# A hybrid decoder trunk: the sliding-window group's norm applied behind the output projection, its tiles placed between the last stick-breaking heads, and a new order at the MLP's opening and end

## The chip, the cores and the metric

The kernel runs on one core of one Trainium2 chip. The metric is the device time of one execution in microseconds (us): the median of three plain runs. Beside them stands one execution taken by the hardware profiler, whose trace is read below. The engines are TensorE (PE; PEld is its weight load), VectorE (DVE), ScalarE (ACT), GpSimd (POOL) and SyncE (SP), which issues nearly all DMAs.

## The reference

Two layers over 512 positions of width 1024, all in float32. In each:

```python
h = rmsnorm(x, attn_norm[l])
proj = h @ w_in[l]                      # sb_q, sb_k, sb_v (8 heads), sw_q (8 heads), sw_k, sw_v (2 heads), 64 wide
sb_o = stick_breaking_attention(...)    # z = q k / 8; a = exp(log_sigmoid(z) + suffix sums of -softplus(z)); a @ v
sw_o = sliding_window_sink_attention(...)   # rotary, window 128, softmax with sinks
mix = concatenate([rmsnorm(sb_o, sb_norm[l]), rmsnorm(sw_o, swa_norm[l])])
x = x + mix @ w_out[l]
h = rmsnorm(x, mlp_norm[l])
x = x + square(relu(h @ w_up[l])) @ w_down[l]
```

and a last rmsnorm. An rmsnorm divides every position (a column, below) by the root of its mean square and multiplies every channel by a gain.

## The kernel before

x lies in SBUF transposed, as 8 chunks of 128 channels by 512 positions. Every product is made of three float32r matmuls on a split of both operands into a high and a low part: high x high, high x low, low x high. A weight tile is loaded by DMA ("raw"), its high part is written by ScalarE, its low part by GpSimd. An operand's high part is written by ScalarE, its low part by VectorE. A dense tile is one PSUM bank of 128 x 512; the output projection's tiles take 12 matmuls each (4 chunks x 3).

The norms of the attention input, of the stick-breaking group and of the MLP are applied behind their products: only the gain goes into the operand, and the result is multiplied by 1/rms of its position, a [128, 512] tile made by a matmul with minus_one over summed squares, Ln and Exp on ScalarE and a refinement on VectorE. The sliding-window (SWA) group alone is normed ahead of its product: MN multiplies its four chunks osw by rms_w.

Each layer's attention part is a hand-written order of steps (ORDER_0, ORDER_1). Each engine walks the whole list and carries out its own steps, in the list's order, so the list is at once the queue of every engine; semaphores tie the queues together. The steps that matter, with a number for the tile, head half or chunk:

- T, U (TensorE): the first and second half of an input tile. TE, TH, TL (VectorE, ScalarE, VectorE): scale it, its high part, its low part. VT, VH, VL: the same for a transposed V tile. In layer 1 tile 17 is the query of heads 6 and 7; in layer 0 it is their V.
- BS, BX, BA (TensorE, L802 to L832): scores, suffix sums and output of the stick-breaking heads. Head h has the halves 2h (768 columns) and 2h+1 (512 columns) for BS and BX, and one BA. Between BS and BX lie BE (ScalarE, Abs, Exp, Ln), BP (VectorE), BH (ScalarE) and BL (VectorE); between BX and BA lie XE, XH (ScalarE) and XL (GpSimd). BO (ScalarE) and BD (VectorE) join the output; GH and GL (L1152, L1578) split it into mix_sb.
- SQ, SA: squares of the SWA group and their sum. NW0, NWE0, NWD0, NWF0: its norm's matmul, Ln and Exp, mean, refinement into rms_w. NS0 and so on: the same for the stick-breaking group, into rms_a.
- MN (VectorE, L1616): osw times rms_w. MH (ScalarE, L1182) and ML (VectorE, L1619): high and low part of chunk n of the SWA group, times its gain. The low part lies in the place of osw.
- OS (TensorE, L836 to L847): one of the 8 output tiles of the SWA group. OE (VectorE, L1625): its add into x.
- CH, CL: the high and low parts of weight pack n; at CL, SyncE also issues the load of pack n+2.

Head 7's scores take the banks of DW (z_last), so BS14 waits until the norm sum NW0 has been read, and BS15 for one of the dense banks. After the list come the 8 output tiles of the stick-breaking group, from mix_sb (on VectorE a multiply by rms_a in PSUM, L1630, a drain, and the add, L1632).

The MLP's order is written likewise (MLP_OPEN, MLP_PAIR, MLP_ON). PL: the 8 plain up tiles; PR, PQ, UH, UL: their relu, square and split. NM, NE, ND: the MLP's norm. MC, MH, ML: sums of activations for a fast scheme that the other up tiles use, and their split. KQ, KP and the other K steps: weight splits on ScalarE and GpSimd; LQ, LU, LD: their loads on SyncE. DF and DE or DX: a down tile and its add into x; DF3 takes the bank that DE0 frees. XC: the next layer's operand and the squares of a chunk. In layer 0's end KN0 to KN2 split the next layer's first weights.

## Time and profile before

| | us |
|---|---|
| median of three plain runs | 1172.91 (1172.42 to 1173.19) |
| profiled execution, own time | 1174.64 |
| its span, first to last instruction | 1172.9 |
| TensorE matmuls busy | 1139.7 |
| TensorE weight loads busy | 995.1 |
| VectorE busy | 829.1 |
| GpSimd busy | 714.2 |
| ScalarE busy | 659.6 |
| granted TensorE clock, mean | 0.994 of 2.4 GHz |

A busy time is the sum of an engine's instructions; matmuls overlap, so a matmul row of 0.39 us can be followed by the next after 0.23. A row of a timeline gives start, duration (of all it merges), engine, line and operands, and in brackets the idle time of the engine before it with what ended that. A name with "q" is the engine's sequencer. Layer 0's attention part ends at about 244 us, its MLP at 588; layer 1's attention part ends at about 818.

### The profile page before, as it was taken

To read this page: it belongs to the slowest core of one execution; us is meant where nothing else is said; L and a number is where in the kernel's file an instruction comes from. 1 tells how busy PE (TensorE), PEld (TensorE's weight loads), DVE (VectorE), ACT (ScalarE), POOL (GpSimd) and SP (SyncE) were. 2 spreads that over 40 slices of the span, in tenths; PEclk is the share of its full clock that TensorE was granted. 3 is DMA by queue.
4 is the path that set the end of the run, shared out by engine and by line. 5 is a ranking of instruction groups with operands and counts; after the bars stand their busy time and mean duration, and the time that the engine had idled before them with its cause. 6 is when DMAs were issued, how large, how long until landed. Compare 5 with 4: busy or idle time off the path is not lost.

```text
span 1172.9 us, 17809 instructions
## 1 busy us (share of the span) xinstructions
PE 1139.7 (97%) x6410; PEld 995.1 (85%) x6410; DVE 829.1 (71%) x1119; ACT 659.6 (56%) x1134; POOL 714.2 (61%) x430
## 2 busy tenths in 40 slices
PE   7999998999999999999999999899999999999996
PEld 5789887877899999989788889788878999999986
DVE  6766677687767778675755766767777877777755
ACT  6789898464344444443546888875643444444333
POOL 3454753674777768774754555556656877767733
PEclk9999998999999999999999999999999999999999
DMA  5220310422242322322222111114323232332222
GB/s 190 73 70 21 91 37 19 144 90 90 90 127 85 109 96 91 126 78 86 67 75 74 54 55 55 37 36 127 108 74 125 90 127 76 104 109 91 86 59 72
DMA packets 30055, 100.01 MB, mean 85 GB/s; under 512 B 3600, under 2 KB 5648, under 8 KB 29968
## 3 DMA queue, kind: packets, MB, share of 16 engines
q1 hardware_dynamic: 28992, 97.80, 26.4%
q8 instruction: 51, 0.84, 0.3%
q10 hardware_dynamic: 976, 1.08, 0.3%
q14 instruction: 36, 0.29, 0.1%
HBM read 96.77 MB, written 2.10 MB: 84 GB/s over the span
## 4 chain that ended last, share of the span: by engine, by line
PE 78%; ACT 8%; DVE 6%; issue 2%; ACTq 1%; DVEq 1%; POOL 1%; DMA 1%; POOLq 0%; SPq 0%
PE DW L672 27%; PE Z L649 5%; PE Z L648 5%; PE Z L647 5%; PE DW L639 5%; PE DW L641 5%; PE DW L640 5%; PE Z L639 3%; PE Z L641 3%; PE Z L640 3%; PE Z L819 2%; PE DW L753 2%; PE DW L649 1%; PE DW L648 1%; PE DW L647 1%
## 5 line engine op out<-in xcount | busy, mean ns | idle before, releaser
L672 PE MATMUL DW<-stage,wx 128*128 128x512 f32 (+1 forms) x816 | 193.3, 388 | 1.6 <-POOL wx L1283 1.6
L672 PEld LDWEIGHTS DW<-stage,wx 128*128 128x128 f32 x816 | 148.6, 188 | 30.2 <-POOL wx L1283 2.0
L672 PE MATMUL DW<-stage,w 128*128 128x512 f32 (+1 forms) x720 | 171.2, 387 | 2.0 <-DVE x L1694 2.0
L672 PEld LDWEIGHTS DW<-stage,w 128*128 128x128 f32 x720 | 130.8, 188 | 27.6 <-DVE x L1694 2.9
L1271 POOL TENSOR_TENSOR w<-raw,w 128x1024 fp32r<-128x1024 f32 x49 | 120.2, 2461 | 53.5 <-ACT w L957 49.7
L1692 DVE TENSOR_TENSOR DW<-DW,probs 128x512 f32<-128x512 f32 x122 | 85.1, 697 | 77.8 <-PE DW L672 74.1
L1289 POOL TENSOR_TENSOR w<-wsum,w 128x512 fp32r<-128x512 f32 x72 | 104.2, 1448 | 42.5 <-ACT w L995 42.5
L639 PE MATMUL DW<-xa,w 128*128 128x512 f32 x296 | 119.3, 403 | 9.4 <-DVE xa L1406 7.2
L1283 POOL TENSOR_TENSOR w<-raw_more,w 128x1024 fp32r<-128x1024 f32 x30 | 73.2, 2441 | 76.8 <-ACT w L977 76.6
L1283 POOL TENSOR_TENSOR wx<-raw_more,wx 128x1024 fp32r<-128x1024 f32 x34 | 82.6, 2433 | 59.1 <-ACT wx L977 58.9
L641 PE MATMUL DW<-xa,w 128*128 128x512 f32 x296 | 116.2, 393 | 0.0
L640 PE MATMUL DW<-xa,w 128*128 128x512 f32 x296 | 116.1, 392 | 0.0
L1289 POOL TENSOR_TENSOR w<-raw,w 128x512 fp32r<-128x512 f32 x60 | 91.4, 1538 | 0.7 <-ACT w L995 0.7
L1694 DVE TENSOR_TENSOR x<-DW,x 128x512 f32<-128x512 f32 x122 | 84.4, 692 | 9.4 <-issue 0.4
L649 PE MATMUL Z<-xm,w 128*128 128x256 f32 x288 | 81.5, 283 | 0.0
L648 PE MATMUL Z<-xm,w 128*128 128x256 f32 x288 | 81.5, 283 | 0.0
L647 PE MATMUL Z<-xm,w 128*128 128x256 f32 x288 | 81.2, 282 | 0.0
L1336 POOL TENSOR_TENSOR stage<-work,stage 128x768 fp32r<-128x768 f32 (+1 forms) x32 | 50.9, 1595 | 44.5 <-ACT stage L1138 43.8
L1429 DVE TENSOR_TENSOR wsum<-raw 128x512 f32<-128x512 f32 x48 | 71.8, 1496 | 7.1 <-issue 4.9
L639 PEld LDWEIGHTS DW<-xa,w 128*128 128x128 f32 x296 | 56.0, 189 | 22.5 <-issue 10.5
L1345 POOL TENSOR_TENSOR probs<-probs,small 128x1024 f32<-128x1024 f32 (+1 forms) x16 | 27.3, 1705 | 74.9 <-DVE small L1597 74.9
L1220 ACT ACTIVATE stage<-kf 128x512 fp32r<-128x512 f32 x64 | 40.6, 634 | 51.6 <-DVE kf L1677 25.6
(327 smaller groups left out, 3104.0 us busy)
## 6 DMA issues: line engine op xcount, KB each, us to landing
raw<-in_weights SPq DMA_DIRECT2D x115, 512.0 KB, 3.7
raw_more<-in_weights SPq DMA_DIRECT2D x64, 512.0 KB, 3.6
x<-in_x SPq DMA_DIRECT2D x6, 256.0 KB, 6.4
out_x<-x SPq DMA_DIRECT2D x6, 256.0 KB, 2.5
raw<-in_weights SPq DMA_DIRECT2D x2, 256.0 KB, 4.4
x<-in_x ACTq DMA_DIRECT2D x2, 256.0 KB, 5.1
out_x<-x ACTq DMA_DIRECT2D x2, 256.0 KB, 2.5
work<-in_positions SPq DMA_DIRECT2D x1, 256.0 KB, 6.0
```

The costliest lines, as they stand in the source:

```text
L639: pe.matmul(bank, slots[slot][:, 0, k], rhs[:, 0, c], start=start, stop=False)
L640: pe.matmul(bank, slots[slot][:, 0, k], rhs[:, 1, c], start=False, stop=False)
L641: mm = pe.matmul(bank, slots[slot][:, 1, k], rhs[:, 0, c], start=False, stop=stop)
L647: pe.matmul(bank, weights_[:, c], part(0, c), start=start and c == 0, stop=False, skip_group_check=not start)
L648: pe.matmul(bank, weights_[:, c], part(1, c), start=False, stop=False, skip_group_check=not start)
L649: mm = pe.matmul(bank, weights_[:, HC + c], part(0, c), start=False, stop=c == HC - 1, skip_group_check=not start)
L672: mm = pe.matmul(bank, weights_[a], part(b, at + c), start=i == c == a == b == 0, stop=i == len(packs) - 1 and c == HC - 1 and a == 1)
L1271: pool.tensor_tensor(slot[:, 1], raw[:, p % 2], slot[:, 0].bitcast(F32), ALU.subtract).then_inc(w_ready, 1)
L1283: pool.tensor_tensor(slot[:, 1], raws[2 + k % 2], slot[:, 0].bitcast(F32), ALU.subtract).then_inc(w_ready, 1)
L1289: pool.tensor_tensor(to[:, HC:], granule_from(kind), to[:, 0:HC].bitcast(F32), ALU.subtract).then_inc(w_ready, 1)
L1692: dve.tensor_tensor(down_bank[n], down_bank[n], rms2, ALU.mult)
L1694: dve.tensor_tensor(x[:, d], down_bank[n], x[:, d], ALU.add).then_inc(d_drained, 1)
```

## The change

The SWA group's norm moves behind its projection. MN is gone; MH and ML work on the raw osw (MH waits for the group's output, ML also for its squares having been read, since it overwrites osw). OE multiplies the output tile in PSUM by rms_w, drains, and adds it into x. In both orders MH and ML stand earlier, MH0, ML0, MH1 and ML1 among the steps of heads 3 to 5, and the OS tiles are spread: OS0 behind BX11, OS1 behind BS14, OS2 behind BS15, OS3 behind BA6, OS4 behind BX15, OS5 behind BA7, OS6 and OS7 behind NS0. NW0 stands behind OS0, BS12 and BX11 ahead of it. The PSUM banks of the OS tiles and the waits for them change with that. The group norm's Ln and Exp (NSE0) stand ahead of GH2 and GH3, and OE5 to OE7 behind the whole of it. In the MLP's opening MC3 and MH3 come ahead of PL4's steps, KQ6 and KQ7 behind UH4 and UH5, and DE0 ahead of UL5; in layer 0's end KP31 comes ahead of DX57 and XC3.

```diff
@@ -86,8 +86,8 @@
 GX0 GX1 LQ2 KQ2 LQ3 KQ3 LQ4 LQ5 MC0 PL0 PR0 MH0 PQ0 UH0 ML0 UL0 KP0 LD2 GX2 PL1 PR1 PQ1 UH1 MC1 UL1 KP1 LD3 MH1 ML1 GX3
-PL2 NM0 KQ4 PR2 PQ2 UH2 MC2 UL2 MH2 NE0 PL3 KQ5 PR3 PQ3 UH3 UL3 ND0 ML2
-LQ6 PL4 KQ6 LQ7 PR4 PQ4 UH4 UL4 PL5 KQ7 LU4 PR5 PQ5 UH5 UL5 MC3 MH3 DF0 DE0 DF1 DE1 KP2 LD4 ML3 DF2 DE2 KA4 KB4 SA4 SB4 DF3 DE3 KP3 LD5 SC4 SD4 KS4 KU4
+PL2 NM0 KQ4 PR2 PQ2 UH2 MC2 UL2 MH2 NE0 PL3 KQ5 PR3 PQ3 UH3 UL3 ND0 ML2 MC3 MH3
+LQ6 PL4 PR4 PQ4 UH4 KQ6 LQ7 UL4 PL5 PR5 PQ5 UH5 KQ7 LU4 DF0 DE0 UL5 DF1 DE1 ML3 KP2 LD4 DF2 DE2 KA4 KB4 DF3 DE3 SA4 SB4 KP3 LD5 SC4 SD4 KS4 KU4
 PL6 KT4 PR6 PQ6 UH6 UL6 PL7 KD4 KV4 LU5 PR7 PQ7 UH7 UL7 DF4 DE4 DF5 DE5 KP4 LD6 DF6 DE6 DF7 DE7
@@ -98,7 +98,7 @@
 MLP_ON = '''
-KP29 LD31 KN0 DF54 DX54 XC0 DF55 DX55 XC1 XS1 KP30 DF56 DX56 XC2 XS2 DF57 DX57 XC3 XS3 KP31 LN2 DF58 DX58 XC4 XS4 KN1 LN3
+KP29 LD31 KN0 DF54 DX54 XC0 DF55 DX55 XC1 XS1 KP30 DF56 DX56 XC2 XS2 DF57 KP31 DX57 XC3 XS3 LN2 DF58 DX58 XC4 XS4 KN1 LN3
 DF59 DX59 XC5 XS5 KN2 LN4 DF60 DX60 XC6 XS6 DF61 DX61 XC7
@@ -186,14 +186,13 @@
 WN5 BA2 TH13 BX6 BX7 TL13 BO2 CH17 WT5 SA2 XE6 CL16 BS8 WH5 U14 BE8 WL5 BD2 XH6 SQ3 BP8 TE14 WS6 BH8 WM6 XE7
-CL17 XL6 XH7 WA5 WE6 WO5 BS9 BL8 T15 WR6 BE9 U15 WN6 TH14 XL7 WT6 BP9 SA3 WH6 TE15 BX8 WD5 WL6 BH9 CH18 SQ4
-CL18 CH19 TL14 BA3 VT15 XE8 BL9 WS7 WM7 BO3 XH8 BS10 T16 BE10 WE7 VH15 BX9 XL8 U16 BD3 WR7 XE9 TE16 WN7 VL15
-BP10 WA6 XH9 WT7 WO6 WD6 TH16 BS11 T17 WH7 WL7 BE11 SQ5 TL16 SA4 WA7 BP11 XL9 CL19 BH10 CH20 SQ6 WO7 SA5 BL10
-WD7 U17 BH11 BL11 BX10 SQ7 GH0 XE10 BA4 TE17 GL0 SA6 SA7 NW0 XH10 BO4 BS12 NWE0 BD4 NWD0 NWF0 BE12 MN0 BX11
-MN1 XL10 XE11 BS13 BP12 XH11 BE13 MN2 BP13 BH12 XL11 MH0 VT17 BL12 BH13 VH17 BA5 MN3 MH1 MH2 ML0 ML1 BL13 BX12
-GH1 MH3 VL17 BS14 BX13 XE12 XH12 ML2 XE13 BS15 BE14 BO5 ML3 BP14 XL12 BE15 XH13 OS0 CL20 BD5 OS1 BP15 BH14
-BH15 XL13 GH2 GL1 CH21 BL14 OS2 OS3 BA6 OE0 BX14 BL15 CH22 OE1 XE14 OE2 GL2 BX15 XE15 XH14 CL21 BO6 CL22 OE3
-CH23 OS4 OE4 XH15 BD6 XL14 OS5 XL15 OE5 CH24 BA7 OS6 CL23 BO7 BD7 CL24 OS7 GH3 OE6 OE7 GL3 NS0 NSE0 NSD0 NSF0
+CL17 XL6 XH7 WA5 WE6 WO5 BS9 BL8 T15 WR6 BE9 U15 WN6 TH14 XL7 WT6 BP9 SA3 MH0 WH6 TE15 BX8 WD5 WL6 BH9 CH18 SQ4
+CL18 CH19 TL14 BA3 VT15 XE8 BL9 ML0 WS7 WM7 BO3 XH8 BS10 T16 BE10 WE7 VH15 BX9 XL8 U16 BD3 WR7 XE9 TE16 WN7 MH1 VL15
+BP10 WA6 XH9 WT7 WO6 WD6 TH16 BS11 T17 WH7 WL7 BE11 SQ5 TL16 SA4 WA7 BP11 XL9 CL19 BH10 CH20 SQ6 WO7 SA5 BL10 ML1
+WD7 U17 BH11 BL11 BX10 SQ7 GH0 XE10 BA4 TE17 GL0 MH2 MH3 SA6 SA7 VT17 XH10 VH17 BS12 BO4 ML2 VL17 BD4 XL10 ML3 BX11 XE11 OS0
+XH11 XL11 BE12 NW0 NWE0 BS13 BP12 NWD0 NWF0 BE13 BA5 BP13 BS14 BH12 BL12 BH13 BL13 OE0 OS1 BO5 BE14 BX12 XE12 BX13 XE13 BD5 BS15 XH12 XL12 BP14 XH13 XL13 BH14 OS2 BL14 BE15 CL20 OE1 BP15
+BX14 XE14 BA6 BH15 BL15 XH14 XL14 OS3 BO6 GH1 GL1 BD6 BX15 XE15 OE2 XH15 XL15 OS4 BA7 CH21 CL21 BO7 BD7 OE3 OS5 CH22 OE4
+NS0 NSE0 NSD0 NSF0 CL22 GH2 GL2 GH3 GL3 CH23 CL23 OE5 OS6 OE6 OS7 OE7 CH24 CL24
 """
@@ -206,15 +205,13 @@
 WL4 VL12 TE13 BP7 WS5 WM5 BH6 BH7 BL6 CL16 BL7 WE5 WR5 XL5 TH13 T14 WN5 U14 WA4 CH18 WO4 SQ3 BX6 WT5 BX7 WH5
-TL13 WD4 BA2 XE6 WL5 SQ4 BO2 XE7 BS8 WS6 BD2 CL17 TE14 WM6 BS9 XH6 BE8 SA3 WE6 BE9 WR6 T15 BP8 BH8 U15 BP9 XH7
-BH9 BL8 WA5 CL18 WO5 XL6 WN6 XL7 WT6 WH6 TH14 CH19 BX8 WD5 BL9 BA3 WL6 BX9 XE8 TL14 BO3 WS7 XH8 BS10 WM7 T16
-CL19 WE7 BE10 TE15 VT15 BD3 WR7 XE9 XH9 WN7 SA4 U16 SQ5 SA5 BP10 WA6 VH15 VL15 WT7 XL8 WO6 XL9 BS11 BH10 WD6
-WH7 SQ6 WL7 T17 WA7 TE16 VT16 CH20 BE11 BL10 BP11 U17 SA6 WO7 VH16 WD7 BH11 SQ7 BL11 SA7 GH0 TE17 TH17 VL16
-TL17 BX10 NW0 XE10 BS12 NWE0 BE12 NWD0 NWF0 BA4 MN0 BX11 MN1 XH10 BO4 XE11 MN2 BS13 BP12 BS14 MN3 MH0 BH12
-BE13 CL20 BL12 ML0 BS15 BX12 GL0 XH11 XL10 BP13 MH1 MH2 BD4 XL11 BH13 BL13 BA5 ML1 MH3 ML2 ML3 BE14 BP14 XE12
-BX13 XE13 BH14 XH12 OS0 BO5 OS1 BL14 OE0 XL12 BE15 BD5 BX14 BP15 XH13 XL13 OS2 GH1 BH15 XE14 BA6 BL15 CH21
-BX15 CL21 XE15 XH14 XL14 OE1 BO6 OS3 GL1 XH15 CH22 GH2 OS4 BD6 GL2 CH23 XL15 OE2 CL22 OE3 BA7 OS5 OE4 BO7 BD7
-OS6 NS0 CH24 OE5 CL23 CL24 NSE0 GH3 OS7 GL3 OE6 OE7 NSD0 NSF0
+TL13 WD4 BA2 XE6 WL5 SQ4 BO2 XE7 BS8 WS6 BD2 CL17 TE14 WM6 BS9 XH6 BE8 SA3 MH0 WE6 BE9 WR6 T15 BP8 BH8 U15 BP9 XH7
+BH9 BL8 WA5 CL18 WO5 XL6 WN6 XL7 WT6 WH6 TH14 CH19 BX8 WD5 BL9 ML0 BA3 WL6 BX9 XE8 TL14 BO3 WS7 XH8 BS10 WM7 T16
+CL19 WE7 BE10 TE15 VT15 BD3 WR7 XE9 XH9 WN7 SA4 MH1 U16 SQ5 SA5 BP10 WA6 VH15 VL15 ML1 WT7 XL8 WO6 XL9 BS11 BH10 WD6
+WH7 SQ6 WL7 T17 WA7 TE16 VT16 CH20 BE11 BL10 BP11 U17 SA6 WO7 VH16 WD7 BH11 SQ7 BL11 MH2 MH3 SA7 GH0 TE17 TH17 VL16
+TL17 BX10 XE10 BS12 BA4 ML2 ML3 BX11 XH10 XL10 XE11 OS0 BO4 XH11 XL11 BE12 NW0 NWE0 BS13 GL0 BD4 BP12 NWD0 NWF0 BE13 BA5 BP13 BS14 BH12 BL12 BH13 BL13 OE0 OS1 BO5 BE14 BX12 XE12 BX13 XE13 BD5 BS15 XH12 XL12 BP14 XH13 XL13 BH14 OS2 BL14 BE15 CL20 OE1 BP15
+BX14 XE14 BA6 BH15 BL15 XH14 XL14 OS3 BO6 GH1 GL1 BD6 BX15 XE15 OE2 XH15 XL15 OS4 BA7 CH21 CL21 BO7 BD7 OE3 OS5 CH22 OE4
+NS0 NSE0 NSD0 NSF0 CL22 GH2 GL2 GH3 GL3 CH23 CL23 OE5 OS6 OE6 OS7 OE7 CH24 CL24
 """
@@ -351,6 +348,11 @@
+def last_plain_in(bank):
+
+    return max(n for n in range(2, PLAIN) if (n - 2) % 3 == bank)
+
+
 def finished(l, step, n):
@@ -379,7 +381,8 @@
         tile_bank[2:4] = [Z3[:, 1], Z3[:, 2]]
-        swa_bank = [D[:, 0], Z3[:, 0], Z3[:, 1], Z3[:, 2]]
+        swa_bank = [D[:, 1], D[:, 0], Z3[:, 0], Z3[:, 1], Z3[:, 2], D[:, 0], Z3[:, 0], Z3[:, 1]]
+        swa_freed_by = {5: 1, 6: 2, 7: 3}
         sb_bank = [D[:, 1], W[:, 1], D[:, 0], Z3[:, 0], Z3[:, 1], Z3[:, 2]]
@@ -529,10 +532,10 @@
         (d_drained, scaled, qk_ready, v_ready, w_drained, sb_sp, sb_split, swa_max, swa_rcp, pt_ready,
-         o_drained, swa_o, sb_o, mw_norm, mw_ready, mb_ready, x_full, xa_ready, xm_ready, mlp_sq, u_ready, angle,
+         o_drained, swa_o, sb_o, mw_ready, mb_ready, x_full, xa_ready, xm_ready, mlp_sq, u_ready, angle,
          start_summed, y_vector, closing_rms, o_joined) = map(sem, (
              "d_drained", "scaled", "qk_ready", "v_ready", "w_drained", "sb_sp", "sb_split",
-             "swa_max", "swa_rcp", "pt_ready", "o_drained", "swa_o", "sb_o", "mw_norm", "mw_ready", "mb_ready",
+             "swa_max", "swa_rcp", "pt_ready", "o_drained", "swa_o", "sb_o", "mw_ready", "mb_ready",
              "x_full", "xa_ready", "xm_ready", "mlp_sq", "u_ready", "angle",
@@ -785,7 +788,7 @@
                             else:
-                                pe.wait_ge(d_drained, l * DENSE + IN_TILES + 1)
+                                pe.wait_ge(d_drained, l * DENSE + SWA_TILE + 3)
                         elif h:
@@ -837,13 +840,15 @@
                         if n == 0:
-                            pe.wait_ge(d_drained, l * DENSE + IN_TILES + 2)
+                            pe.wait_ge(d_drained, l * DENSE + IN_TILES + 1)
                             pe.wait_ge(mw_ready, l * SWA_CHUNKS + SWA_CHUNKS)
                         elif n == 1:
+                            pe.wait_ge(d_drained, l * DENSE + IN_TILES + 2)
+                        elif n == 2:
                             pe.wait_ge(z_drained, l * PIECES + 2 * LAST_HEAD + 1)
-                        elif n >= len(swa_bank):
-                            pe.wait_ge(d_drained, l * DENSE + tile - len(swa_bank) + 3)
-                        products(slot_of(p), swa_bank[n % len(swa_bank)], mix_swa, range(PAIRS), n % 2 * PAIRS, True, True
+                        elif n in swa_freed_by:
+                            pe.wait_ge(d_drained, l * DENSE + SWA_TILE + swa_freed_by[n] + 3)
+                        products(slot_of(p), swa_bank[n], mix_swa, range(PAIRS), n % 2 * PAIRS, True, True
                                  ).then_inc(tile_done, 1)
@@ -851,7 +856,8 @@
                     if d > 1:
-                        pe.wait_ge(d_drained, l * DENSE + tile - len(sb_bank) + 3)
+                        freed_by = tile - len(sb_bank) if d > 5 else SWA_TILE + min(d + 3, KC - 1)
+                        pe.wait_ge(d_drained, l * DENSE + freed_by + 3)
                     products(slot_of(p), sb_bank[d % len(sb_bank)], mix_sb, range(PAIRS), d % 2 * PAIRS, True, True,
@@ -880,14 +886,14 @@
                                 pe.wait_ge(mlp_relu, relu_count(l, 2 * n - 4))
-                            elif n == FIRST_PAIR:
-                                pe.wait_ge(d_drained, drained(l, "PL", PLAIN - 2))
+                            else:
+                                pe.wait_ge(d_drained, drained(l, "PL", last_plain_in(n % 2)))
                             up_product(acc_a[n % 2], granule("A", n), lambda h, c: xm[:, h, c, 0:HALF], True)
...
                             else:
-                                pe.wait_ge(d_drained, drained(l, "PL", PLAIN - 1))
+                                pe.wait_ge(d_drained, drained(l, "PL", last_plain_in(2)))
                             up_product(acc_b, granule("B", n), lambda h, c: xm[:, h, HC + c, 0:HALF], True)
@@ -1170,6 +1176,10 @@
                         act.activation(other[DH:P, 0:2 * P], O[0:DH, 2 * P:T], ACT.Identity).then_inc(o_moved, 1)
+                    elif step == "MH":
+                        act.wait_ge(swa_o, l * SWA_STEPS + n // 2 * NB + NB)
+                        act.activation(mix_swa[:, 0, n], osw[:, n], ACT.Identity,
+                                       scale=gain_of(l, KC + PAIRS + n)).then_inc(mw_hi, 1)
                     elif step == "SQ":
@@ -1177,10 +1187,6 @@
                                        ).then_inc(swa_sq, 1)
-                    elif step == "MH":
-                        act.wait_ge(mw_norm, l * SWA_CHUNKS + n + 1)
-                        act.activation(mix_swa[:, 0, n], osw[:, n], ACT.Identity,
-                                       scale=gain_of(l, KC + PAIRS + n)).then_inc(mw_hi, 1)
@@ -1612,17 +1618,18 @@
                         dve.drain().then_inc(swa_o, 1)
-                    elif step == "MN":
-                        dve.tensor_tensor(osw[:, n], osw[:, n], rms_w[:, :], ALU.mult).then_inc(mw_norm, 1)
                     elif step == "ML":
                         dve.wait_ge(mw_hi, l * SWA_CHUNKS + n + 1)
+                        dve.wait_ge(swa_sq, l * SWA_STEPS + n // 2 * NB + NB)
                         dve.scalar_tensor_tensor(mix_swa[:, 1, n], osw[:, n], gain_of(l, KC + PAIRS + n),
...
                         dve.wait_ge(tile_done, l * DENSE + tile + 1 + CREDIT)
-                        dve.tensor_tensor(x[:, n], swa_bank[n % len(swa_bank)], x[:, n], ALU.add).then_inc(d_drained, 1)
+                        dve.tensor_tensor(swa_bank[n], swa_bank[n], rms_w[:, :], ALU.mult)
+                        dve.drain()
+                        dve.tensor_tensor(x[:, n], swa_bank[n], x[:, n], ALU.add).then_inc(d_drained, 1)
                 for d in range(KC):
```

## Rows read from the trace of the kernel before

**Rows 1.** The page's part 1: busy us, share of span, instructions of each engine.

```profile
PE 1139.7 (97%) x6410; PEld 995.1 (85%) x6410; DVE 829.1 (71%) x1119; ACT 659.6 (56%) x1134; POOL 714.2 (61%) x430
```

**Rows 2.** TensorE's waits, whole span: who for whom, us, times, longest.

```profile
PE DW L672 <- DVE x L1694: 2.0, 2, 1.0
...
PE DW L672 <- POOL wx L1283: 1.6, 1, 1.6
```

**Rows 3.** Timeline, TensorE, layer 1: start, us, engine, line, output<-inputs [idle before].

```profile
750.20 0.51 PE L819 MATMUL Z<-stage,minus_tri 128*128 128x384 f32 x2
...
751.64 1.07 PE L678 MATMUL DW<-acc,minus_one 128*128 128x512 f32 x2
753.98 1.00 PE L802 MATMUL Z<-xm 128*128 128x384 f32 x6 [1.27 <-DVE xm L1523]
...
755.04 1.45 PE L832 MATMUL O<-stage,xm 128*128 128x512 f32 x8
756.32 0.68 PE L819 MATMUL Z<-stage,minus_tri 128*128 128x512 f32 x2
...
760.10 0.74 PE L802 MATMUL Z<-xm 128*128 128x512 f32 x2 [2.34 <-ACT work L1132]
...
796.73 0.39 PE L639 MATMUL DW<-xa,w 128*128 128x512 f32 x1
```

**Rows 4.** The same in layer 0.

```profile
173.12 0.40 PE L641 MATMUL DW<-xa,w 128*128 128x512 f32 x1
173.35 0.51 PE L819 MATMUL Z<-stage,minus_tri 128*128 128x384 f32 x2
...
182.22 1.22 PE L802 MATMUL Z<-xm 128*128 128x512 f32 x2 [2.80 <-ACT work L1132]
...
222.17 0.40 PE L640 MATMUL DW<-xa,w 128*128 128x512 f32 x1
```

**Rows 5.** Windows: length, each engine's busy us (instructions), then granted clock, DMA, GB/s.

```profile
181.00:192.00 11.00, 9.32 (x36) 8.46 (x36) 9.91 (x14) 9.94 (x16) 1.28 (x1) 0.53 0.01 2
```

**Rows 6.** Single lines: shortest/median/longest ns, first and last start, for MH, ML, MN, L1630.

```profile
L1182 ACT ACTIVATE stage<-osw,gains x8: 707/712/715, 186.2 to 765.6; 128x512 fp32r<-128x512 f32 x8
...
L1619 DVE SCALAR_TENSOR_TENSOR stage<-osw,gains,stage x8: 744/746/752, 187.8 to 767.7; 128x512 fp32r<-128x512 f32 x8
...
L1616 DVE TENSOR_TENSOR osw<-osw,rms_w x8: 684/689/1502, 181.7 to 759.8; 128x512 f32<-128x512 f32 x8
...
L1630 DVE TENSOR_TENSOR DW<-DW,rms_a x10: 686/700/700, 226.0 to 818.8; 128x512 f32<-128x512 f32 x10
```

**Rows 7.** Timeline, ScalarE, layer 0: XH10.

```profile
176.27 0.84 ACT L1138 ACTIVATE stage<-work 128x768 fp32r<-128x768 f32 x1 [0.35 <-PE O L832]
```

**Rows 8.** Timeline, ScalarE and VectorE, layer 1: GH0, TH17, TL17.

```profile
750.46 0.73 ACT L1152 ACTIVATE xa<-o,gains 128x512 fp32r<-128x512 f32 x1 [0.43 <-PE DW L641]
...
751.21 1.20 ACT L1087 ACTIVATE xm<-DW 64x512 fp32r<-64x512 f32 x2
...
752.44 1.39 DVE L1523 TENSOR_TENSOR xm<-DW,xm 64x512 fp32r<-64x512 f32 x2 [0.67 <-ACT xm L1087]
```

**Rows 9.** Timeline, layer 0's MLP opening: end of ML2, start of MC3, DE0, DF3.

```profile
277.32 0.68 DVE L1655 TENSOR_TENSOR xa<-DW,xa 128x512 fp32r<-128x512 f32 x1
...
283.53 0.43 DVE L1645 TENSOR_TENSOR O<-gx 128x256 f32<-128x256 f32 x1
...
285.61 0.70 DVE L1692 TENSOR_TENSOR DW<-DW,probs 128x512 f32<-128x512 f32 x1
...
287.13 3.04 PE L672 MATMUL DW<-stage,w 128*128 128x512 f32 x12 [1.02 <-DVE x L1694]
```

**Rows 10.** Timeline, end of layer 0: XC3's first instruction, KP31 on GpSimd, DF60's second half.

```profile
574.31 0.72 ACT L1018 ACTIVATE xa<-x,gains 128x512 fp32r<-128x512 f32 x1 [3.04 <-DVEq L1696]
...
577.16 2.37 POOL L1283 TENSOR_TENSOR wx<-raw_more,wx 128x1024 fp32r<-128x1024 f32 x1 [0.18 <-issue]
...
579.58 3.02 PE L672 MATMUL DW<-stage,wx 128*128 128x512 f32 x12 [1.61 <-POOL wx L1283]
```

## The prediction

> **What bounds the kernel now.** I read the page first. TensorE is busy for 97% of the span, the next engine for 71% [rows 1]; so the end is set by TensorE, and the change can only give back time in which TensorE stands still or runs slowly. TensorE's list of waits comes next: it says that such time is short and lies in few places. Two of those lie in the MLP: one wait of 1.6 us on GpSimd's split of the last down weights, and one of 1.0 us in each layer on VectorE's add into x [rows 2]. The largest lie between the last stick-breaking heads. There the stretch from the first sum of head 5 (BX10) to the first tile of the stick-breaking group's output projection has to be compared with its work.
>
> The work at full clock, from the starts of neighbouring steps in layer 1 [rows 3]: a BX half 1.44 us (750.20 to 751.64), a first BS half 1.06, a BA 1.28; a second BS half is shorter, 0.65 (2 of 512 columns and one of 128, estimated from its columns). A matmul of 512 columns starts every 0.227 us (173.12 to 173.35 is 0.23, [rows 4]; 12 of them are 2.72), so eight output tiles are 21.8. A norm sum, including the slow matmul that follows, is taken as 1.25. The stretch holds 6 BX, 4 BA, 2 + 2 BS halves, 2 norm sums, 8 tiles: 8.6 + 5.1 + 3.4 + 2.5 + 21.8 = 41.5 us, and 42.1 in layer 0, which has a transposed V tile inside (0.6). Measured: layer 0 from 173.35 to 221.94 (222.17 less one pitch, [rows 4]) is 48.6, so 6.5 are lost; layer 1 from 750.20 to 796.73 [rows 3] is 46.5, so 5.0 are lost. In layer 0 one wait is 2.80 long [rows 4], and the granted clock of the 11 us around it is 0.53, so nearly all of it stood at 1.2 GHz [rows 5]; in layer 1 the waits are 1.27 and 2.34 [rows 3], and the clock stays at 2.4 GHz.
>
> Everything recoverable is then 6.5 + 5.0 + 1.6 + 2 x 1.0 = 15 us, 1.3%.
>
> **The change part by part.** I count against the profiled execution: span 1172.9, own time 1174.64; the median of the plain runs is 1172.91, so its own time lies 1.7 above what is to be predicted, and I take the difference off the median.
>
> *Scaling after the projection.* Eight MN leave VectorE (0.69 each, up to 1.50, [rows 6]); each of sixteen OE gets a multiply in PSUM (0.70, the same form as L1630, [rows 6]) and a drain. OE grows from 0.7 to 1.45 us. Tiles follow each other by 2.72, so VectorE keeps up: free, except that OE0 must now follow the norm and frees the bank of BS15, and that OE5 to OE7 lie behind the norm of the other group. By my walk OE7 ends 1.6 us after the first SB tile, and the SB loop needs 2.35 us of VectorE in 2.72 of TensorE, so the lag is gone before the MLP. Cost 0, bound 1.
>
> *MH0, MH1, ML0, ML1 move earlier.* ScalarE has 0.71 us more at each of two places (taken as 0.62 where instructions overlap), VectorE 0.75 [rows 6]. No step of it is on TensorE's path, but ScalarE is full there. I take 0.4 for layer 0 and 0.6 for layer 1, where MH1 stands before all that feeds the last input tile; bounds 0 and 1.4 (both instructions whole).
>
> *Layer 0, what is late next.* TensorE: BX10, BA4, VT17, BS12, BX11, done at 179.2. OS0 now stands here and needs all four ML. ScalarE does XE10, MH2, MH3, XH10 (0.84, [rows 7]), VH17 (0.6, as one of TH17's two, [rows 8]), ending at 178.6; VectorE has VL17 and BD4 queued ahead of ML3 (0.7 each) and VL17 waits for VH17: 178.6 + 0.7 + (BO4) 0.8 + 0.75 = 181.0. So TensorE waits 1.8 us in front of OS0. What is queued behind it is NW0, so ScalarE's norm and BE13 wait also. Then OS0, BA5, BS14, OS1 cover the norm (1.3 on ScalarE, 2.9 on VectorE) and the split of head 6. Head 7 comes out 1.0 late for BX14 (BD5's three instructions stand ahead of BP14, OS2 covers 2.7), OS2 itself 0.2, and NS0 0.5: from BA7's end BO7, BD7, the square and the add take some 3.2, and only OS5 (2.7) lies over them where OS6 and OS7 did before. Sum 1.8 + 1.0 + 0.2 + 0.5 + 0.4 = 3.9 instead of 6.5: **-2.6**.
>
> *Layer 1.* Its last input tile is the query of heads 6 and 7, so BS12 waits for TL17. In the trace GH0 starts at 750.46, TH17 at 751.21, TL17 at 752.44, BS12 at 753.98 [rows 3, 8]. MH2 and MH3 are now put ahead of GH0: 750.03 (GH0's start less its 0.43 idle) + 1.3, GH0 0.7, TH17 1.2, TL17 1.4 gives 754.7, with the 0.6 from above 755.3. NW0 (1.1) no longer fills the gap and BA4 stands behind BS12. TensorE is idle for 3.1 us after BX10 (seen against its own shifted start), where 1.27 plus NW0 stood. The later wait of 2.34 goes, as do the smaller ones before OS0, as OS0 and OS1 cover them. Left over: 3.1 + 0.6 + 0.6 (small ones at BX12 and OS2) + 1.2 (BX14) + 0.5 (NS0) = 6.0 instead of 5.0: **+1.0**.
>
> *Opening of the MLP.* DF3 starts at 287.13 after a wait of 1.02 for DE0 [rows 9]. MC3 leaves the place before DE0 and UL5 too, but MC3 (2.1 us, 283.53 to 285.61) goes in front of PQ4, and MH3 goes in front of PR4 on ScalarE, KQ6 in front of PR5. From the end of ML2 (278.0, [rows 9]): MC3 2.1, MH3 1.1, PR4 0.6, PQ4 0.7, UH4 0.6, KQ6 0.95, PR5 0.6, PQ5 0.7 makes 285.4; DE0 1.5 ends at 286.9. DF2 ends at 286.1. The wait shrinks from 1.0 to 0.8: **-0.15** a layer, bounds 0 and -1.0. The loads LQ7 and LU4 and the splits KQ7, KA4, KB4 go some 6 us later; the first product that needs them is at about 312, after DF7, so they stay hidden; if that cover were gone, KA4 alone would cost its lateness.
>
> *KP31.* GpSimd splits it from 577.16 to 579.53, and DF60's second half waits for it until 579.58 [rows 10]. Its slot is free after DF57. ScalarE was idle for 3.04 before XC3 [rows 10], so its part runs there, and GpSimd takes it at 574, done by 576.4, before 577.97 where TensorE comes to it. **-1.6**. Late next is the last xa chunk, which has 1.5 us of slack.
>
> *Waits on banks (the changed swa_bank, sb_bank and last_plain_in).* Each is released well before, 0.
>
> Sum: -2.6 + 1.0 - 0.3 - 1.6 = -3.5, so 1174.6 becomes 1171.1 for the profiled one, and the median 1172.9 - 3.5 = **1169.4**. With the bounds of these terms (2 us on each tail's walk) 1165.5 to 1173.
>
> **The clock, weighed.** In layer 0 a wait of 2.80 went with a clock of 1.2 GHz, in layer 1 a wait of 2.34 did not [rows 3, 4, 5]. My walk leaves 1.8 in layer 0 and 3.1 in layer 1, and behind both TensorE's queue is now dense. If the clock falls after the layer 1 gap for as long as it did in layer 0 (0.53 over 11 us), about 5 us of work take 10; 0.5 of that is taken up by later waits: +4.5, so 1173.9.
> The Trainium skill ("TensorE: Matmul & The Clock Gate", section "HAM oscillation") states that a wait in front of the matmuls throttles them and that the next burst starts cold. By that rule the gap in layer 1 costs this, and a shorter gap in layer 0 might free what it costs now; the layer 0 rows agree with it, the 2.34 of layer 1 shows that not every gap counts.
>
> **The rivals.**
> A: the clock falls behind one of the two gaps (layer 1 above all): 1173.9, no difference that can be measured. For it: 3.1 is longer than the 2.80 that had it. Against: the walk's 3.1 is uncertain by 1. Chance 0.24.
> B, slower: it falls behind both, the dense queue after OS0 in layer 0 as well (+4.6): 1178.5. It decides from the point at which OS0's wait nears the 2.8 of layer 0 before; VL17 and BD4 ahead of ML3 are its place. A walk that is 1 us short makes it so. 0.15.
> C: the chains run tighter than my walk (the order keeps ScalarE full, SBUF-only MN no longer stretch next to GpSimd): of the 15 us, 8 come back: 1165. For it: ScalarE needs only some 29 us between BX10 and NS0, TensorE 35. 0.14.
> D: the change doesn't do what it says at the last heads: tiles only move the waits, layer 0 gains nothing, and KP31 and the opening alone are left, with layer 1's +1: 1172. 0.09.
> Forecast 0.38.
>
> **How the numbers follow.** About 0.2% (2.3 us) is what a measurement of this kernel can tell from no change: faster means below 1170.6, slower above 1175.3. Forecast: about 0.31 of 0.38 lies below 1170.6, the rest same. C is faster (0.14); A is mostly same (0.04 of it slower, 0.03 faster); B slower; D same. Faster 0.48, same 0.33, slower 0.19. The range of 8 in 10 takes in C, A and part of B: 1164.5 to 1177.
>
> **What would show it.** Right: waits on KP31 gone; a wait of about 3 us before BS12 in layer 1, with GH0 and TH17 later; OS0 in layer 0 waiting for VectorE's ML3; about 0.8 us before DF3. Wrong: a PEclk digit under 9 near 755 (A), two of them (B), tails of 43 to 44 us from BX10 to the first SB tile (C; forecast 46.0 and 47.5). A new wait later than 290 us in the MLP for KA4 or LU4's load would break the zero that I gave them.

## The result and the profile after

| | us |
|---|---|
| kernel after, median of four runs | 1188.59 (1186.25 to 1189.86) |
| kernel before, median of four | 1172.97 (1172.42 to 1173.19) |
| ratio | 1.0119, 95% interval 1.0101 to 1.0137 |
| profiled execution, own time / span | 1188.9 / 1187.2 |

It is slower by 1.2%, 15.6 us; the forecast was 1169.4, in a range of 1164.5 to 1177. Both are missed, and the side with them. The sections below show why: the new order puts VectorE's instructions beside GpSimd's weight splits, and there VectorE stands still. Line numbers of the kernel after are 3 higher on TensorE (L642 is the first of the three matmuls of a product), 5 to 7 higher elsewhere.

The head of the page of the kernel after answers to [rows 1]:

```profile
span 1187.2 us, 17843 instructions
...
PE 1144.8 (96%) x6410; PEld 994.5 (84%) x6410; DVE 846.0 (71%) x1127; ACT 658.1 (55%) x1134; POOL 717.2 (60%) x430
```

TensorE is busy for 5.1 us more and stands still for the rest of the 14.3 us of span. VectorE is busy for 16.9 us more, with some 5.5 us of new work (16 multiplies in the place of 8 MN, 0.69 each). TensorE's waits, from the list of the kernel after (us in total, times, longest):

```profile
PE DW L675 <- DVE x L1701: 3.3, 4, 0.9
PE Z L805 <- DVE xm L1529: 2.8, 1, 2.8
PE DW L642 <- DVE stage L1624: 2.5, 1, 2.5
PE Z L642 <- POOL w L1283: 1.9, 1, 1.9
PE DW L642 <- DVE xa L1584: 1.8, 1, 1.8
...
PE O L780 <- DVE pt L1607: 1.6, 1, 1.6
PE DW L642 <- DVE x L1701: 1.3, 1, 1.3
```

Left out above them is the wait of 7.1 for the first operand, which the kernel before has too (7.2). Set against [rows 2] and the waits of 2.80 and 2.34 in [rows 4] and [rows 3], the wait for KP31 and those two are gone, and the ones shown are new or longer, none over 2.8 us. Comparing the starts of the matmul of the same number in the two traces tells where the time goes. After minus before (times of the kernel before) is -0.6 in layer 0's first stick-breaking (SB) tile (223), +3.3 at 228, +4.2 at 309, +3.8 at 720 in layer 1, +5.2 at 743, +6.9 at BX10 (750.20), +7.9 at 754, +8.8 at layer 1's first SB tile (797), +10.4 at its first plain up tile (818), +13.4 at 847 and +14.3 at the end. So the loss is in many steps of 1 to 4 us, and most of it lies outside the stretch that the prediction walked through.

The largest step of layer 0, in VectorE's timeline of the kernel after (start, duration, brackets: idle before it):

```profile
220.96 4.50 DVE L1584 SCALAR_TENSOR_TENSOR xa<-o,gains,xa 128x512 fp32r<-128x512 f32 x2
...
226.93 0.69 DVE L1630 TENSOR_TENSOR Z<-Z,rms_w 128x512 f32<-128x512 f32 x1
```

GpSimd's timeline beside it:

```profile
219.74 2.40 POOL L1277 TENSOR_TENSOR w<-raw,w 128x1024 fp32r<-128x1024 f32 x1 [2.05 <-ACT w L963]
222.34 2.57 POOL L1277 TENSOR_TENSOR w<-raw,w 128x1024 fp32r<-128x1024 f32 x1 [0.20 <-ACT w L963]
226.65 2.38 POOL L1277 TENSOR_TENSOR w<-raw,w 128x1024 fp32r<-128x1024 f32 x1 [1.74 <-ACT w L963]
```

and TensorE's:

```profile
225.51 0.50 PE L642 MATMUL DW<-xa,w 128*128 128x512 f32 x1 [1.80 <-DVE xa L1584]
```

GL2 and GL3 take 4.50 us together, where one such instruction takes 0.75 when GpSimd is idle, so 1.5 for the two: the pair ends only 0.55 behind the second split. The multiply at 226.93, which has one of its inputs in PSUM, takes its usual 0.69 beside the third split. In the kernel before GL3 ran at 221.88 and took 0.74, GpSimd being idle:

```profile
224.56 2.40 POOL L1271 TENSOR_TENSOR w<-raw,w 128x1024 fp32r<-128x1024 f32 x1 [5.67 <-ACT w L957]
```

In layer 1 ML1 is caught (VectorE, GpSimd and TensorE of the kernel after):

```profile
748.25 2.36 DVE L1624 SCALAR_TENSOR_TENSOR stage<-osw,gains,stage 128x512 fp32r<-128x512 f32 x1 [0.22 <-issue]
```

```profile
748.20 3.55 POOL L1342 TENSOR_TENSOR stage<-work,stage 128x768 fp32r<-128x768 f32 x2 [0.24 <-issue]
```

```profile
748.23 0.47 PE L642 MATMUL DW<-xa,w 128*128 128x512 f32 x1 [0.96 <-DVEq L1551]
752.80 1.22 PE L780 MATMUL O<-pt,vsw 128*128 128x256 f32 x8 [1.58 <-DVE pt L1607]
761.44 1.00 PE L805 MATMUL Z<-xm 128*128 128x384 f32 x6 [2.78 <-DVE xm L1529]
```

and in the MLP's opening of layer 1 the second instruction of MC1, 0.48 elsewhere, starts together with the split KP1 and ends 0.3 behind it:

```profile
843.33 2.69 DVE L1653 SCALAR_TENSOR_TENSOR DW<-x,gains,gx 128x256 f32<-128x256 f32 x1
```

```profile
843.33 2.39 POOL L1289 TENSOR_TENSOR w<-raw_more,w 128x1024 fp32r<-128x1024 f32 x1 [0.21 <-ACT w L983]
```

```profile
859.99 0.50 PE L642 MATMUL Z<-xm,w 128*128 128x512 f32 x1 [1.88 <-POOL w L1283]
```

MC1 delays MH1, MC2 and MH2, and behind MH2 on ScalarE stands KQ5, whose split TensorE waits for; the page names GpSimd, the cause is on VectorE 17 us earlier.

The granted clock behind three of the waits (columns: stretch, us, busy time of PE, PEld, DVE, ACT and POOL, PEclk, DMA share, GB/s):

```profile
182.00:186.00 4.00, 4.00 (x11) 3.17 (x12) 0.96 (x1) 1.69 (x2) 0.97 (x1) 0.57 0.00 0
226.00:231.00 5.00, 5.00 (x17) 3.91 (x16) 4.70 (x8) 1.63 (x2) 3.59 (x2) 0.66 0.98 333
762.00:767.00 5.00, 5.00 (x25) 4.56 (x24) 1.58 (x3) 1.03 (x2) 1.15 (x1) 0.66 0.00 0
```

In each TensorE works for a part of the stretch at 1.2 GHz, and loses 4.00 x 0.43 = 1.7, 5.00 x 0.34 = 1.7 and 1.7 us. Three of them are 5.1 us. The slower clock is thus a part of what a wait costs (1.8 becomes 3.5 at layer 0's first SB tile).

The profiled execution of the kernel before lost 11 x 0.47 = 5.2 in one long stretch in layer 0 and nothing in layer 1 [rows 5]. It is not typical of its kernel. Six runs below have the same order of attention steps. Five of them (e2_mlp, e3_kp31, e6_bquiet, e9_oe, g5_kp1mh2) have a clock of 0.84 in the same 11 us, a loss of 1.8, and each has a second slow stretch in layer 1, behind the same wait of 2.3. The sixth, g1_kp1, has the long stretch too, in a profiled execution that is 2.3 us above its own median. The windows of e3_kp31:

```profile
181.00:192.00 11.00, 8.82 (x46) 7.58 (x46) 9.99 (x15) 10.12 (x17) 1.29 (x1) 0.84 0.01 2
759.00:763.00 4.00, 4.00 (x20) 3.81 (x18) 3.73 (x6) 3.78 (x7) 0.92 (x1) 0.57 0.00 0
```

and that of the kernel before in layer 1:

```profile
759.00:763.00 4.00, 2.90 (x17) 2.58 (x18) 3.83 (x5) 3.84 (x7) 1.70 (x1) 1.00 0.00 0
```

From BX10 to the first SB tile of layer 0 these five take 46.5 to 47.0 us, the profiled execution of the kernel before 48.6, and the kernel after 47.5. So set against its usual executions the kernel before lost 1.7 us less in this stretch than [rows 4] show, and the new order gained nothing there: it is 0.5 to 1 us longer.

The theory to be tested, called S: VectorE's instructions with both inputs in SBUF (GL, ML, UL, MC) stand still while GpSimd's subtraction of two SBUF operands runs; the new order puts such instructions of TensorE's path beside splits. The rivals: D, late loads and late low parts of weights; M, the new MLP lists; L, each place costs what its own wait shows, and a repair gives it back; and the multiplies in OE.

### The profile page after: what moved, and what is told of

Its sections match the earlier page's. It is cut to its first block, busy times and chain, and to the rows that moved or that the text cites. A ratio compares the mean times of both kernels' runs of the same rounds, so it can differ in the third digit from the quotient of the medians.

```text
span 1187.2 us, 17843 instructions
## 1 busy us (share of the span) xinstructions
PE 1144.8 (96%) x6410; PEld 994.5 (84%) x6410; DVE 846.0 (71%) x1127; ACT 658.1 (55%) x1134; POOL 717.2 (60%) x430
## 4 chain that ended last, share of the span: by engine, by line
PE 70%; DVE 13%; ACT 8%; DVEq 3%; issue 2%; ACTq 2%; DMA 1%; POOL 0%
PE DW L675 24%; PE Z L652 5%; PE Z L651 5%; PE Z L650 5%; PE DW L642 4%; PE DW L644 4%; PE DW L643 4%; PE Z L822 2%; PE DW L756 2%; PE O L835 1%; PE Z L642 1%; PE Z L644 1%; PE Z L643 1%; ACTq L1124 1%; DVE x L1701 1%
## 5 line engine op out<-in xcount | busy, mean ns | idle before, releaser
L642 PE MATMUL DW<-xa,w 128*128 128x512 f32 x296 | 120.2, 406 | 12.9 <-DVE xa L1412 7.1
L1342 POOL TENSOR_TENSOR stage<-work,stage 128x768 fp32r<-128x768 f32 (+1 forms) x32 | 53.5, 1681 | 51.9 <-ACT stage L1144 51.2
L642 PEld LDWEIGHTS DW<-xa,w 128*128 128x128 f32 x296 | 56.5, 191 | 26.8 <-issue 12.4
L1012 ACT ACTIVATE o<-Z 128x256 f32<-128x256 f32 x48 | 18.4, 384 | 89.2 <-PE Z L652 89.2
```

The source lines that it names most:

```text
L642: pe.matmul(bank, slots[slot][:, 0, k], rhs[:, 0, c], start=start, stop=False)
```

## Experiments: which part of the change

**Attention part alone** (e1_attn): the kernel after with MLP_OPEN and MLP_ON as they were.

```diff
-PL2 NM0 KQ4 PR2 PQ2 UH2 MC2 UL2 MH2 NE0 PL3 KQ5 PR3 PQ3 UH3 UL3 ND0 ML2 MC3 MH3
+PL2 NM0 KQ4 PR2 PQ2 UH2 MC2 UL2 MH2 NE0 PL3 KQ5 PR3 PQ3 UH3 UL3 ND0 ML2
...
-DF57 KP31 DX57 XC3 XS3 LN2
+DF57 DX57 XC3 XS3 KP31 LN2
```

> The kernel after with the MLP's two lists (its opening and layer 0's end) as they were: the attention part's change alone. Theory L (losses add up by place): by the starts of equal matmuls in the two traces the attention parts lose 3.3 in layer 0 and 6.5 in layer 1, so 1172.9 + 9.8 = 1182.7. Theory I (interaction: the attention part's late loads and splits hurt only the new opening order): 1176 or less. Theory M (the new MLP lists are to blame for most): 1176 or less, and the other kernel, with the MLP lists alone, is near 1185.

Measured 1187.05 (1182.57 to 1187.79), ratio 1.0105 (1.0081 to 1.0129). **MLP lists alone** (e2_mlp): the same lines the other way, in the kernel before.

> The kernel before with the new MLP opening and the earlier KP31, no change to the attention part. Theory L: layer 0's opening +0.9, KP31 -1.8 with 1.5 given back at layer 1's second input tile, layer 1's opening up to +3.9: together +4.5, 1177.4. Theory I: the opening costs nothing where loads and splits come as early as before; with the earlier KP31 it is 1172 to 1173, and the wait of TensorE for KP31 is gone from the trace.

Measured 1175.47, ratio 1.0013 (1.0002 to 1.0025). M falls as the main cause: the attention part alone loses as much as the whole change, within the intervals, and even its fastest execution (1182.57, at a mean clock of 0.996; the other three stand at 0.991 to 0.992) lies 9.2 above the kernel before. At that clock it is 3.7 below the fastest of the kernel after (1186.25, at 0.995), so the lists may cost a few us on the new attention order; on the old one they cost 2.1 by the medians and gain nothing.

**KP31 alone** (e3_kp31):

```diff
-DF57 DX57 XC3 XS3 KP31 LN2
+DF57 KP31 DX57 XC3 XS3 LN2
```

> The kernel before with KP31 alone moved ahead of DX57 and XC3. Forecast of the prediction: -1.6, 1171.4. Reading of the trace of the kernel after: the wait for KP31 goes (-1.8), and 1.3 to 1.5 come back at the second input tile of layer 1, which waits for the last add into x to free its bank: 1172.6 to 1172.9, no difference that can be measured. In the kernel with the new MLP lists alone TensorE was 2.1 earlier at the end of layer 0 and 0.7 later at the end of layer 1's stick-breaking heads.

Measured 1173.81 beside 1173.32, ratio 1.0001 (0.9991 to 1.0012). Its TensorE row at layer 1's second input tile:

```profile
588.62 0.47 PE L639 MATMUL DW<-xa,w 128*128 128x512 f32 x1 [1.34 <-DVE x L1694]
```

KP31's wait of 1.6 is gone, and 1.34 of it stands here: the tile's PSUM bank is free only after the last add into x. That add is late because VectorE's low part of a chunk of xa, 0.75 elsewhere, stands ahead of it beside a split of the next layer's first weights. VectorE and GpSimd of e3_kp31:

```profile
585.09 2.00 DVE L1406 SCALAR_TENSOR_TENSOR xa<-x,gains,xa 128x512 fp32r<-128x512 f32 x1 [0.90 <-ACT xa L1018]
```

```profile
584.15 2.40 POOL L1370 TENSOR_TENSOR w<-raw,w 128x1024 fp32r<-128x1024 f32 x1 [0.18 <-issue]
```

At 0.75 the add would end 1.25 earlier, which is nearly the whole wait (an estimate from these rows; no run tests it).

**The multiplies of OE alone** (e9_oe), in the kernel before (MN stays, so the norm is applied twice):

```diff
+                        dve.tensor_tensor(bank, bank, rms_w[:, :], ALU.mult)
+                        dve.drain()
```

> The kernel before, in which every OE also multiplies its tile in PSUM by rms_w and drains, as in the kernel after (MN is kept, so the norm is applied twice: the price of sixteen multiplies on VectorE alone). Prediction: 0, bound 1. Rival: VectorE's 0.77 more for each tile holds up NW's refinement, BP and BL of the last heads or the norm of the other group: 2 us or more slower, 1175 or above.

Measured 1175.99, ratio 1.0020 (1.0007 to 1.0033). In its trace TensorE is 2.0 ahead of the kernel before until 841 in layer 1, 1.6 of it by the shorter slow stretch in layer 0. There it falls back by 4.3, of which a shorter wait behind it returns 1.3. The rows of VectorE, GpSimd and TensorE:

```profile
830.69 2.68 DVE L1649 SCALAR_TENSOR_TENSOR DW<-x,gains,gx 128x256 f32<-128x256 f32 x1
```

```profile
830.69 2.39 POOL L1283 TENSOR_TENSOR w<-raw_more,w 128x1024 fp32r<-128x1024 f32 x1 [0.21 <-ACT w L977]
```

```profile
847.37 0.71 PE L639 MATMUL Z<-xm,w 128*128 128x512 f32 x1 [1.86 <-POOL w L1277]
```

The multiplies cost nothing where they stand: layer 0's stretch from BX10 is 47.0, layer 1's 46.5, as in the runs without them. A small shift of VectorE against GpSimd brings MC1 beside KP1, and this costs 1.9 of waiting and 1.7 at 1.2 GHz (the granted clock is 0.50 from 847.5 to 850.5).

## Experiments: contention, delay or load

**Quiet GpSimd in the kernel after** (e5_quiet): a memset, which reads nothing, instead of the subtraction.

```diff
+                if p > 20:
+                    pool.memset(slot[:, 1].bitcast(F32), 0.0).then_inc(w_ready, 1)
+                    return
                 pool.tensor_tensor(slot[:, 1], raw[:, p % 2], slot[:, 0].bitcast(F32), ALU.subtract).then_inc(w_ready, 1)
...
-                pool.tensor_tensor(slot[:, 1], raws[j % 2], slot[:, 0].bitcast(F32), ALU.subtract).then_inc(w_ready, 1)
+                pool.memset(slot[:, 1].bitcast(F32), 0.0).then_inc(w_ready, 1)
```

> The kernel after, but GpSimd writes the low parts of the weight packs 21 to 25, of the plain up tiles and of the first four down tiles with a memset that reads nothing (so these low parts are zero and the sums leave them out). Nothing else is changed. Theory S: VectorE's GL, UL and MC instructions beside them fall back to 0.75, 0.69 and 0.49 each; GL2 and GL3 together take 1.5 instead of 4.5; TensorE's waits at the first SB tile of layer 0, at PL4, PL5 of layer 1 go: 5 to 8 us faster than the kernel after (1181 to 1184). Rival D (the loads set the time, not VectorE): the instructions shrink but the waits stay for raw or w, under 2 us faster. A part of a gain may be the 1.4 us that each split itself is shorter; the trace tells which (waits on w against waits on xa, O, DW).

Measured 1174.98 (1173.83 to 1175.92): 13.6 less than the kernel after, where 5 to 8 were expected. **Quiet GpSimd in the kernel before** (e6_bquiet), the same edit:

> The control to the quiet kernel: the kernel before with the same memsets in place of GpSimd's splits of the packs 21 to 25, of the plain up tiles and of the first four down tiles (their low parts are zero and left out of the sums). The quiet form took 13.6 us off the kernel after (1188.6 to 1175.0). Theory S (the splits beside VectorE's SBUF instructions are what the change made costly): the kernel before gains little by it, 1 to 4 us, 1169 to 1172, so most of the difference between the two kernels goes. Rival G (shorter splits help any order by their 1.4 us each): the kernel before gains 8 us or more, under 1165, and the difference of 15 stays at 10 or more.

Measured 1169.63, ratio 0.9969 (0.9959 to 0.9980). **As long as a split, but without reading** (e7_long):

```diff
+                for _ in range(2):
+                    pool.memset(slot[:, 1].bitcast(F32), 0.0)
+                    pool.drain()
+                pool.memset(slot[:, 1, 0:KC // 2].bitcast(F32), 0.0).then_inc(w_ready, 1)
```

> The quiet kernel after, with each of its memsets replaced by two and a half of them (a drain between), so that GpSimd is busy and each low part comes as late as with the real splits (2.4 us and a little more), but GpSimd reads nothing from SBUF. Tells contention from delay. Theory S: VectorE's GL, UL and MC stay at their short times, 1 to 3 us above the quiet kernel, 1176 to 1178. Rival D (the late low parts set the time): back to 1185 or more with VectorE's instructions short.

Measured 1176.55 (1175.65 to 1178.05). GL2 and GL3 and GpSimd beside them in e7_long:

```profile
222.05 1.61 DVE L1599 SCALAR_TENSOR_TENSOR xa<-o,gains,xa 128x512 fp32r<-128x512 f32 x2
```

```profile
220.82 2.03 POOL L1279 MEMSET w<- 128x1024 f32 x2 [1.79 <-ACT w L963]
222.97 0.53 POOL L1281 MEMSET w<- 128x512 f32 x1
223.58 2.03 POOL L1279 MEMSET w<- 128x1024 f32 x2
```

GpSimd is as busy as with the splits, and the pair takes 1.61 instead of 4.50. So it is GpSimd's reading that holds VectorE up. Of the kernel after's time 12.0 us (1188.6 to 1176.6) are this contention, and only 1.6 the lateness of the low parts: D falls. The kernel before loses 3.3 to 3.7 us to the splits, delay and contention together (1173.3 or 1173.0 to 1169.6). Between the quiet kernels 5.4 of the 15.6 us are left (1174.98 less 1169.63); so some 10 are what the change lost by placing VectorE's instructions beside the splits; by contention alone it is at least 8.3 (12.0 less 3.7). Both traces have a mean clock of 0.995, so they can be set against each other place by place. In layer 0 the new order has lost 1.0 by the first SB tile; the earlier KP31 gains 0.3; in layer 1 1.5 are lost up to T17, 1.6 at WA7 (ML1), and 1.8 from BX10 to the first SB tile.

The Trainium skill states this rule ("SBUF — State Buffer", section "Who interferes with whom"): a VectorE instruction with two SBUF inputs contends with a GpSimd instruction that reads SBUF, not with one that only writes it, and the one that comes second blocks until the first is done. The rows agree with each half of it: 2.69 beside 2.39 from the same start, 0.69 with one input in PSUM, 1.61 beside memsets. GpSimd is held up in its turn where VectorE came first: the split at 222.34 began while GL2 still ran, and took 2.57 instead of 2.40.

**ML1 of layer 1 moved** (e8_ml1), out of the way of XL8 and XL9, which the quiet kernels kept:

```diff
-CL19 WE7 BE10 TE15 VT15 BD3 WR7 XE9 XH9 WN7 SA4 MH1 U16 SQ5 SA5 BP10 WA6 VH15 VL15 ML1 WT7 XL8 WO6 XL9 BS11 BH10 WD6
+CL19 WE7 BE10 TE15 VT15 BD3 WR7 XE9 XH9 WN7 SA4 MH1 U16 SQ5 SA5 BP10 WA6 VH15 VL15 WT7 XL8 WO6 XL9 BS11 BH10 WD6
...
-TL17 BX10 XE10 BS12 BA4 ML2 ML3 BX11
+TL17 BX10 XE10 BS12 BA4 ML1 ML2 ML3 BX11
```

> The kernel after with one step of layer 1 moved: ML1 from behind VL15, where it took 2.36 beside GpSimd's XL8 and XL9, to just ahead of ML2. Theory S: the wait of TensorE of 1.6 ahead of WA7 in layer 1 goes and BX10 comes 1.5 to 2 earlier; OS0 is not held up by the 0.75 more in front of ML3, since BS12 waits longer for TL17: 1187. Rival: ML2, ML3 and TL17's chain take it back, within 0.5 of the kernel after.

Measured 1186.01 (1183.45 to 1190.24), ratio 1.0105 (1.0080 to 1.0130). In the profiled execution the wait of 1.58 ahead of WA7 is gone and 1.6 us are gained there. The clock doesn't fall behind BS12's wait in this execution, and so the stretch from BX10 to the first SB tile takes 46.8 instead of 48.5; e7_long, whose clock stays up there too, has 46.9. At layer 1's first SB tile GL2 and GL3 now stand beside a split (a wait of 1.8), and MC1 no longer does: the shift by 1.6 has moved the collision. The whole time is 2.6 lower, within the spread of both kernels.

## Experiments: can it be repaired

**GL2, GL3 ahead of the norm's VectorE part** (e4_gl), in both layers:

```diff
-NS0 NSE0 NSD0 NSF0 CL22 GH2 GL2 GH3 GL3 CH23
+GH2 GL2 NS0 NSE0 GH3 GL3 NSD0 NSF0 CL22 CH23
```

> The kernel after with GH2, GL2 ahead of NS0 and GH3, GL3 behind NSE0, ahead of ND's part of the norm on VectorE (both layers). Theory S (a VectorE instruction with both inputs in SBUF stands still while GpSimd splits a weight, and GL2, GL3 are on TensorE's path): the wait of 1.8 at the third chunk of layer 0's first SB tile goes, and the slow-clock stretch behind it (1.7) with it: 3 to 4 us faster than the kernel after, 1185. Rival N: the wait only moves to NSF0 or to the next weight, since the loads are late anyway: within 1 us of 1188.6.

Measured 1187.80 (1186.99 to 1189.57): no gain, as rival N has it. In the trace GL2 and GL3 are short, the wait at layer 0's first SB tile is gone (+0.2 against the kernel before at 223 and no step behind it), and at 272 it is +4.1. VectorE and TensorE of e4_gl:

```profile
259.60 2.68 DVE L1653 SCALAR_TENSOR_TENSOR DW<-x,gains,gx 128x256 f32<-128x256 f32 x1
```

```profile
268.64 0.50 PE L642 MATMUL Z<-xm,wx 128*128 128x512 f32 x1 [0.48 <-POOL wx L1283]
276.29 0.50 PE L642 MATMUL Z<-xm,w 128*128 128x512 f32 x1 [1.90 <-POOL w L1283]
```

The collision of MC1 and KP1 has come to layer 0 with the shift; MC1's second instruction was 0.48 there in the kernels before and after. L falls: taking away one wait did not give its time back.

**Three repairs together** (f3_back): the old MLP lists, the edits of e4_gl and of e8_ml1.

> The attention part of the kernel after with three repairs together: the MLP's two lists as before, GL2 and GL3 ahead of the norm's VectorE part, ML1 of layer 1 just ahead of ML2. Each takes a stretched VectorE instruction off TensorE's path. If the places add up: 1187.05 (attention part alone) less 3.9 and 3.9 at the two first SB tiles and 2.5 ahead of WA7: 1177. If a removed wait is met again at the next weight (as when GL2, GL3 alone were moved): 1182 to 1185.

Measured 1185.10, ratio 1.0088 (1.0058 to 1.0117), the number for a wait that is met again. TensorE waits for KQ5 at 276.00 and at 857.17, 1.87 and 1.86 us. **MH1 to MH3 behind TH17 as well** (f1_mh):

```diff
-WN7 SA4 MH1 U16 SQ5
+WN7 SA4 U16 SQ5
...
-BL11 MH2 MH3 SA7 GH0 TE17 TH17 VL16
-TL17 BX10
+BL11 SA7 GH0 TE17 TH17 VL16 MH1 MH2 MH3
+TL17 BX10
```

> As the kernel with three repairs, and in layer 1 MH1, MH2, MH3 on ScalarE behind TH17 too. The theory for layer 1 in the prediction (MH2, MH3 ahead of GH0 and TH17 delay TL17 and so BS12; MH1 delays T17): BS12's wait of 2.8 shrinks to 1.5, T17's wait of 1.0 to under 0.5: 1.5 to 2 us faster than that kernel. Rival: ML3 and OS0 or XE10, BX11 take the wait over, within 0.5.

Measured 1186.13 (1185.02 to 1186.51), no faster. TensorE's waits in it:

```profile
747.56 0.47 PE L642 MATMUL DW<-xa,w 128*128 128x512 f32 x1 [0.35 <-DVEq L1551]
759.85 1.17 PE L805 MATMUL Z<-xm 128*128 128x384 f32 x6 [3.47 <-ACT work L1138]
```

T17's wait falls from 0.96 to 0.35, so MH1 cost 0.6 there. BS12 no longer waits for TL17 (2.78), but for XE10 behind MH3, 3.47: ScalarE has no room for them here.

**Weight steps earlier at the last heads** (f2_cl), on top of f1_mh:

```diff
-BP13 BS14
+BP13 CL20 BS14
...
-XL13 BH14 OS2 BL14 BE15 CL20 OE1 BP15
+XL13 CH21 CL21 BH14 OS2 BL14 BE15 OE1 BP15
...
-XH14 XL14 OS3
+XH14 XL14 CH22 CL22 OS3
```

> As the kernel with MH1 to MH3 late, and the weight packs' steps at the last heads earlier in both layers: CL20 ahead of BS14, CH21 and CL21 ahead of OS2, CH22 and CL22 ahead of OS3. Theory W (part of the loss is that the SB tiles' weights come late: ScalarE waits 2 to 3 us for each raw load from CH23 on, and GpSimd's splits then lie beside xm's low parts): ScalarE's waits for raw shrink and PL0 comes 2 us or more earlier in both layers: 2 to 4 us faster than the kernel without it, near or under 1173. Rival: GpSimd's splits now lie beside BL13 to BL15, which are SBUF only and stand on the heads' chain: no faster, or slower.

Measured 1189.94 (1188.42 to 1191.20), slower by 3.8. BX14 waits 1.84 at 203.02 in the place of 0.61: BL14, SBUF only, and CH21 ahead of BH14 stand on the last heads' chain.

**KP1 behind MH1** so that its split starts when MC1 is done, with e4_gl's edit (g4_glkp1), in the kernel after (g3_akp1), and in the kernel before (g1_kp1):

```diff
-MC1 UL1 KP1 LD3 MH1 ML1 GX3
+MC1 UL1 MH1 KP1 LD3 ML1 GX3
```

> The kernel after with GL2, GL3 ahead of the norm's VectorE part, and KP1 behind MH1 in the MLP's opening, so that GpSimd's split of KP1 starts only when MC1 is done. Theory M (the wait taken away at the first SB tile came back as MC1 beside KP1): both are gone now, so 3 to 4 us faster in layer 0 and up to 4 in layer 1 than with GL alone (1187.8): 1180 to 1184. Rival N (TensorE meets the late weight loads at the next place anyway): within 1 us of 1187.8.

> The kernel after with KP1 behind MH1 alone. Theory M: in layer 0 nothing changes (there GL2, GL3 had the wait and MC1 was not hit), in layer 1 MC1 goes from 2.69 back to 0.49 and the waits at PL4 and PL5 (0.6 and 2.0) go: 2 to 3 us faster than 1188.6. Rival N: within 1 us.

> The kernel before with KP1 behind MH1 alone. In its trace MC1 is not hit (0.48), so no gain is due from MC1; UL1 and UL2 (1.53 and 1.77 instead of 0.69) are off TensorE's path. Theory M: within 1 us of 1173. If it is 2 us or more faster, the kernel before paid for this collision too, and a better kernel than both is found; if 2 us or more slower, the later split of KP1 or KQ4 costs by itself and the two runs on the kernel after understate the gain.

Measured: g4_glkp1 1187.08 (1186.00 to 1189.39), g3_akp1 1193.80 (1187.83 to 1193.86), g1_kp1 1176.72, ratio 1.0026 (1.0016 to 1.0036). No gain by theory M in any of them; g4_glkp1 has the number of its rival N, and g1_kp1 that of its third reading, a cost of the later splits by themselves. MC1 is 0.48 now, but KP1 and KQ4 are split back to back and MC2's first instruction (1.24 in the kernel before) is caught. In layer 0 of g1_kp1 KQ5's high part comes 1.8 later than before: 1.0 is this stall, and 0.8 is ScalarE, which now does KP1's and KQ4's high parts in a row ahead of the relu that MC2 stands behind. **All repairs** (g2_best) has it too: f3_back's, KP1 behind MH1, MH1 beside MH2, BA4 ahead of BS12.

```diff
-TL17 BX10 XE10 BS12 BA4 ML1 ML2 ML3 BX11
+TL17 BX10 XE10 BA4 BS12 ML1 ML2 ML3 BX11
```

> All repairs on the new attention order: the MLP's lists as before but KP1 behind MH1, GL2 and GL3 ahead of the norm's VectorE part, and in layer 1 MH1 and ML1 beside MH2 and ML2 and BA4 ahead of BS12, to fill TL17's wait. From the kernel with three repairs (1185.1): -3.1 and -3.5 for MC1 and KP1 in the two layers, -0.6 for MH1 at T17, -1.3 for BA4: 1176.6. If under 1172.9, the new order can beat the kernel before; my expectation is that it stays 2 to 4 above.

Measured 1182.99 (1182.09 to 1184.03), ratio 1.0075 (1.0060 to 1.0090), some 6 above what was expected. BS12's wait is 2.05, T17's 0.36. VectorE and TensorE of g2_best:

```profile
265.07 2.23 DVE L1652 TENSOR_TENSOR O<-gx 128x256 f32<-128x256 f32 x1
```

```profile
274.70 0.50 PE L642 MATMUL Z<-xm,w 128*128 128x512 f32 x1 [1.91 <-POOL w L1283]
```

**KP1 behind MH2 instead**, in GpSimd's idle time ahead of KQ5, in g2_best (g6_best2) and in the kernel before (g5_kp1mh2):

```diff
-PL2 NM0 KQ4 PR2 PQ2 UH2 MC2 UL2 MH2 NE0
+PL2 NM0 KQ4 PR2 PQ2 UH2 MC2 UL2 MH2 KP1 LD3 NE0
```

> The repaired attention order (MLP lists as before, GL2 and GL3 ahead of the norm's VectorE part, in layer 1 MH1 and ML1 beside MH2 and ML2 and BA4 ahead of BS12) with KP1 behind MH2 instead of behind MH1, so that its split lies in GpSimd's idle time ahead of KQ5. Theory S: MC1 0.5 and MC2 1.1 to 1.3, TensorE's wait of 1.9 for KQ5 goes in both layers: 2 to 5 us faster than with KP1 behind MH1 (1183.0): 1178 to 1181. Rival N (the wait at the plain up tiles has another cause): within 1 us of 1183.

> The kernel before with KP1 behind MH2 alone. Theory S: MC1, MC2 are no longer than now and UL2 shrinks from 1.77 to 0.69, off TensorE's path: within 1 us of 1173, and up to 2 us faster if MC2's 1.2 shrinks and what waits for it is on the path. Rival: ScalarE's extra 1.06 ahead of the norm, or KP1's split just ahead of KQ5's, delays KQ5: 1175 or more.

Measured: g6_best2 1185.81 (1184.58 to 1189.41); g5_kp1mh2 1177.69 (1174.27 to 1181.26), ratio 1.0033 (1.0017 to 1.0048). Both miss theory S; g5_kp1mh2 has the number of its rival. In g6_best2 MC1 and MC2 are 0.48 and 1.43, and the wait for KQ5 is still 1.58: this one is no stall of VectorE. ScalarE now does KP1's high part (1.06) ahead of the norm and of KQ5's, and GpSimd's split of KP1 ends just ahead of KQ5's. The norm's last step (ND, SBUF only) is caught by KQ6. VectorE, GpSimd and TensorE of g6_best2:

```profile
278.29 2.71 DVE L1694 TENSOR_TENSOR probs<-probs 128x512 f32<-128x512 f32 x1
```

```profile
278.05 2.40 POOL L1283 TENSOR_TENSOR wx<-raw,wx 128x1024 fp32r<-128x1024 f32 x1 [3.55 <-ACT wx L972]
```

```profile
291.48 4.61 PE L675 MATMUL DW<-stage,w 128*128 128x512 f32 x12 [3.04 <-DVE x L1701]
```

Three placements of KP1 gave three different victims: MC1, MC2, ND. No version here that does all the work beats the kernel before. The control g1_kp1 is slower by 3.5 us by the medians. Its profiled execution is 4.4 behind that of the kernel before: 1.2 in its first 15 us and 0.4 in layer 0's last heads, both ahead of the edit, then 1.8 at KQ5 in layer 0 and 1.2 in layer 1. That of g5_kp1mh2 has the span of the kernel before, 1172.9, only because it spent less time at 1.2 GHz in layer 0's last heads; at KQ5 it loses 1.0 and 0.8. What its executions of 1179 to 1181 had, at a clock of 0.989 to 0.993, is open.

## Why the prediction was wrong, point by point

The step that failed is the price of the moved steps: each of VectorE's was taken at the time that it has alone ("Cost 0, bound 1" for the scaling with what stands behind it, 0.4 and 0.6 for MH and ML), and the shift that the order gives to all later steps was priced at nothing. In its place the runs show VectorE standing still beside GpSimd's splits: at least 8.3, some 10, of the 15.6 us. The second step that failed is the -2.6 of layer 0: it was measured on an execution whose clock was slow for 1.7 us more than usual, and the new order gained nothing there.

- **OS0 in layer 0 waits for ML3**: right in place and cause, 2.48 instead of 1.8 us. "VL17 and BD4 queued ahead of ML3" is what the trace shows. The clock fell behind it and cost 1.7. BX10 to the first SB tile is 47.5 (173.88 to 221.36) where 46.0 was forecast and 48.6 was before; but in five of the six other runs with the old order it is 46.5 to 47.0. The -2.6 is +0.5 to +1. The prediction took 1.7 off its result because the profiled execution was slower than the plain ones, and didn't ask in which stretch those 1.7 lay; they lay in the very stretch from which it took its largest gain.
- **BS12 in layer 1 waits for TL17**: right, 2.78 instead of 3.1. The tail from BX10 is 48.5 (757.06 to 805.52), forecast 47.5. Without the slow clock behind BS12's wait it is 46.8 and 46.9 (e8_ml1, e7_long), so the walk came out well and the clock cost 1.6.
- **MH and ML moved earlier, 0.6 in layer 1**: the mechanism was seen, the size was not. MH1 costs 0.6 at T17 (its wait falls from 0.96 to 0.35 in f1_mh), as forecast; ML1, priced at 0.75 and off the path, took 2.36 beside XL8 and XL9 and held WD6, WL7 and WA7: 1.6 more. The bound of 1.4 was too low, since it took each instruction at its time when nothing is beside it, though the prediction's own [rows 6] show an MN of 1502 ns where the median is 689.
- **"OE... cost 0, bound 1"**: right for the multiplies (e9_oe). But the steps that went with them were not priced: GL2 and GL3 stand behind the norm with CL22 to CL24 beside them. This was the largest missed term: 3.9 us in layer 0 of the kernel after (-0.6 to +3.3), and 3.9 in each layer of e1_attn.
- **"The lag is gone before the MLP"**: wrong in layer 1, where 1.6 us were lost from the first SB tile to PL0 (+8.8 to +10.4). VectorE has hardly any idle time from there to PL0, and one low part of xm takes 2.39 at 815.33, 0.75 elsewhere, beside the split at 814.76; the quiet kernel after loses nothing there.
- **Opening of the MLP, -0.15**: DF3 waits 0.81 where 1.02 stood, as forecast (0.8), but a second wait of 0.86 came before another down tile (313.12), and the attention part's shift brought MC1 beside KP1's split in layer 1.
- **KP31, -1.6**: the wait went, "late next is the last xa chunk, which has 1.5 us of slack" failed. Late next was the bank of the second input tile, 1.34, behind a low part of xa that a split held up.
- **The rivals**: A and B, the clock, priced a real mechanism. A's place, behind BS12's wait in layer 1, was right, the size was not: 1.6 instead of 4.5, since 4.5 was taken from the one long slow stretch. Another drop, which no rival had, came behind the new wait at layer 0's first SB tile (1.7). C argued that MN no longer stretches next to GpSimd. That was the right mechanism, seen from one side: what goes away beside GpSimd was counted, what comes beside it was not. No rival had this loss.

Of the 15.6 us, some 10 are VectorE's stalls beside the replaced splits, the later low parts and the clock behind them (difference of the two quiet pairs). The other 5.4 are, by the traces of the quiet pair, 1.6 the same stall at ML1, 0.6 MH1, 0.9 more in layer 1 ahead of T17, 1.8 in layer 1's tail, most of it the clock, and 1.0 in layer 0 up to the first SB tile, less 0.3 for KP31 (5.6 in all by the traces). What the 0.9 are is not settled.

## What to carry to other kernels

Before a step with both inputs in SBUF is moved, on VectorE, look at what GpSimd runs at its new time, and bound it by its own duration plus that of GpSimd's instruction; then look at what the shift does to all later pairs of the two engines, since they are tied only through other engines and slide past each other. A change that saves TensorE 2 us moves everything behind it, and a wait that is removed can come back at the next such pair. What would avoid the stall is a GpSimd step that doesn't read SBUF beside VectorE's critical steps, or a VectorE operand kept in PSUM. No run here does this with all the work done; the 3.3 to 3.7 us that the kernel before gained with its low parts left out (e6_bquiet) are a bound for it there.

Before a gain is read from one profiled execution, compare its time with the plain runs. Where it is slower, look for the stretch that is slow in it alone: other runs whose kernel is the same up to that point show it.

## What the runs showed of the hardware

- A VectorE instruction that waits for GpSimd doesn't run slowly, it stands until GpSimd's instruction is over: MC1's second instruction, 0.48 elsewhere, took 2.68 or 2.69 in three kernels (the kernel after, e4_gl, e9_oe), beside a split of 2.39 that began with it.
- A wait of 1.80 (first SB tile) or 1.86 (e9_oe, 847.37) was followed by a stretch at 1.2 GHz, one of 1.88 (kernel after, 859.99) was not: the clock was 1.00 from 860.5 to 863.5. The wait of 2.34 in layer 1 was followed by 1.00 in the profiled execution of the kernel before and by 0.57 in e3_kp31. The length of the wait alone doesn't decide.
- Slow stretches differ between executions in length too: behind the same wait of 2.80 in layer 0 the clock was 0.53 over 11 us in the kernel before and 0.84 in five of six other runs. Where TensorE waits soon after anyway, a slow stretch costs nothing: layer 1's tail is 46.5 with one (e3_kp31) and without (the kernel before).
- Executions of one kernel fall in groups by granted clock: of the kernel before beside e6_bquiet, 24 at 0.994 or above take 1172.7 to 1174.6, and four at 0.990 to 0.991 take 1176.4 to 1176.6. In e8_ml1 two executions at 0.994 and 0.997 took 1183.5, two at 0.991 1188.6 and 1190.2. So e8_ml1 and the kernel after (1186.25 at 0.995, 1188.28 and 1189.86 at 0.992) are better compared at one clock than by medians of four.
